# Two FFN down products as seven block products, with the sums for them and for gate and up on GpSimd

## The reference, cut to what matters

```python
D_MODEL = 1024
FFN_DIM = 2816

def swiglu_half(x, pre, post, w_gate, w_up, w_down):
    h = rmsnorm(x, pre)
    y = (jax.nn.silu(h @ w_gate) * (h @ w_up)) @ w_down
    return x + 0.5 * rmsnorm(y, post)

def layer(x, ...):
    h = swiglu_half(x, W['ffn1_pre'], W['ffn1_post'], W['ffn1_gate'], W['ffn1_up'], W['ffn1_down'])
    ...                                    # time mixing, latent attention, memory attention
    y = swiglu_half(h, W['ffn2_pre'], W['ffn2_post'], W['ffn2_gate'], W['ffn2_up'], W['ffn2_down'])
```

## Time and profile before

| | us |
|---|---|
| median of three executions | 3128.83 (3127.26 to 3136.36) |
| the profiled execution, its own time | 3137.18 |
| its span (first to last instruction) | 3135.5 |
| TensorE busy | 2997.9 (96% of the span) |
| VectorE / ScalarE / GpSimd busy | 1674.7 / 1183.5 / 346.8 |
| mean granted clock of TensorE | 0.981 |

### The profile page before, as it was taken

The page is one execution under the profiler, slowest core; times in us unless marked ns, Lnnn a source line. Parts: engine busy times, 40 slices in busy tenths (PEclk is TensorE's granted clock), DMA queues, the critical chain, the costliest instruction groups (busy, mean ns, idle before and its releaser), DMA issues. The chain is left out here.

```text
span 3135.5 us, 63709 instructions
## 1 busy us (share of the span) xinstructions
PE 2997.9 (96%) x26970; PEld 2836.4 (90%) x26970; DVE 1674.7 (53%) x2830; ACT 1183.5 (38%) x2244; POOL 346.8 (11%) x356
## 2 busy tenths in 40 slices
PE   8999999999999988878899989999998999999998
PEld 8999999999999978838777569999998999999998
DVE  7655554554545556566554552343425755565453
ACT  5333334553112233244665351221243433334444
POOL 3000000112001123230003000000015100000111
PEclk9999999999999999989999999999998999999999
DMA  6222237663422120011015641112123222225764
GB/s 173 82 72 73 80 102 230 205 193 108 142 71 68 48 89 4 18 27 45 13 46 166 221 169 51 51 44 61 31 77 99 82 82 82 75 82 176 222 186 138
DMA packets 419542, 312.53 MB, mean 100 GB/s; under 512 B 45720, under 2 KB 391105, under 8 KB 418490
## 3 DMA queue, kind: packets, MB, share of 16 engines
q1 hardware_dynamic: 414394, 288.98, 30.6%
q0 software_dynamic: 3824, 19.47, 1.8%
q10 hardware_dynamic: 1040, 0.00, 0.0%
HBM read 249.20 MB, written 59.21 MB: 98 GB/s over the span
## 5 line engine op out<-in xcount | busy, mean ns | idle before, releaser
L2033 PE MATMUL banks<-hid_pieces,dn_part 128*128 128x344 f32 x3168 | 501.9, 320 | 2.0 <-DVE dn_part L1998 1.3
L2033 PEld LDWEIGHTS banks<-hid_pieces,dn_part 128*128 128x128 f32 x3168 | 498.3, 188 | 3.0 <-DVE dn_part L1998 1.7
L1802 PE MATMUL banks<-x_pieces,gate_pieces 128*128 128x258 f32 x3360 | 414.3, 283 | 0.0
L1802 PE MATMUL banks<-x_pieces,up_pieces 128*128 128x258 f32 x3360 | 414.1, 283 | 0.0
L1802 PEld LDWEIGHTS banks<-x_pieces,gate_pieces 128*128 128x128 f32 x3360 | 408.6, 189 | 0.0
L1802 PEld LDWEIGHTS banks<-x_pieces,up_pieces 128*128 128x128 f32 x3360 | 408.6, 189 | 0.0
L1167 PEld LDWEIGHTS banks<-XR,pR 128*128 128x128 f32 (+1 forms) x1800 | 284.2, 188 | 10.3 <-issue 6.1
L1167 PE MATMUL banks<-XR,pR 128*128 128x344 f32 (+1 forms) x1800 | 289.6, 322 | 3.6 <-DVE pR L2509 2.9
L2012 DVE TENSOR_TENSOR dn_part<-dn_raw,dn_part 128x768 fp32r<-128x768 f32 (+1 forms) x188 | 173.7, 938 | 217.4 <-ACT dn_part L2006 217.4
L1167 PE MATMUL banks<-XR,mg_gate 128*128 128x344 f32 x1728 | 283.3, 319 | 1.3 <-PEq L53 1.3
L1167 PEld LDWEIGHTS banks<-XR,mg_gate 128*128 128x128 f32 x1728 | 273.8, 188 | 1.6 <-issue 1.6
(11 more groups left out here) (523 smaller groups left out, 4744.2 us busy)
## 6 DMA issues: line engine op xcount, KB each, us to landing
dn_raw<-in_ffn_down SPq DMA_DIRECT2D x94, 384.0 KB, 3.5
dn_raw<-in_ffn_down SPq DMA_DIRECT2D x94, 320.0 KB, 3.2
hid_spill<-h_stage SPq DMA_DIRECT2D x44, 516.0 KB, 3.4
hid_raw<-hid_spill SPq DMA_DIRECT2D x24, 688.0 KB, 4.9
praw<-in_w_in SPq DMA_DIRECT2D x24, 512.0 KB, 4.2
sq<-in_w_in SPq DMA_DIRECT2D x24, 512.0 KB, 4.1
tiles<-h_spill SPq DMA_DIRECT2D x8, 1376.0 KB, 8.7
gu_raw<-in_ffn_gate SPq DMA_DIRECT2D x20, 512.0 KB, 4.0
```

What stands on the lines that cost most here:

```text
L1802: ins = k.nc.tensor.matmul(out, self.w[m][:, a, w, f * P:(f + 1) * P], self.x[p][:, b, x, f * TQ:(f + 1) * TQ], start=first and f == 0 and ...
L2033: ins = k.nc.tensor.matmul(k.ps[j][:, 0:TG], w[a][:, f * P:(f + 1) * P], k.hid_pieces[h][:, b, f, :], start=h == 0 and f == 0 and r == 0, ...
```

## The change

- **Down as seven block products.** The output is cut 2 by 2 (tiles 0 to 3 and 4 to 7; columns 0 to 515 and 516 to 1031), and the hidden tiles in even and odd ones. Seven products `m` of the table `DOWN` take the place of eight, in 32 units: units 0 to 23 hold four output tiles of a product for two quarters of 258 columns, the last eight one quarter each. That makes 7 x 4 x 2 x 33 = 1848 matmuls of 258 columns where 1584 of 344 were.
- **Operands for it.** A block product takes weights A11, A12, A22 (blocks of the down weights) or sums S1 to S4 of them, and hidden blocks B11, B21, B22 or sums T1 to T4. `chain` makes, for one pair of hidden tiles, four S or four T on GpSimd: three loads issued by GpSimd itself, three sums with a store to DRAM (`w_sums`, `t_sums`) behind each, a fourth load, a fourth sum and its store. All wait for one another through three buffers. `chains` runs one S and one T chain for each of the 11 iterations, 22 in all, in each FFN.
- **The gate and up weight sums** move from VectorE to GpSimd (`w_sums_pool`), into the same stream; the raw loads now also wait for them.
- **Evictions.** Products 0 and 1 are copied out by ScalarE, products 2 to 6 are added to what is there by VectorE. Squares, norms and the loads around them move to other places (`SQUARES`, `between`), and the split input of the projections gets another layout (`XG`).
- **A new wait of SP**: in `sp_down` the load of the last hidden part of product 1 stands behind `chain_sums.wait(sp, 2 * self.CHAIN)`, all 88 sums of the chains, since that part takes the place of a chain buffer. ScalarE waits for all stores of the chains at unit 5.

```diff
+    H_PARTS = ((0, 0, 5), (0, 5, 9), (0, 9, 11), (1, 0, 6), (1, 6, 11))
     DN_PARTS = ((0, 6), (6, 11))
+    DOWN = (("A11", "B11"), ("A12", "B21"), ("S2", "T2"), ("S3", "T3"), ("A22", "T4"), ("S1", "T1"), ("S4", "B22"))
+    FRESH = (0, 2, 3, 5)
+    UNITS = [(m, j, (0, 1)) for m in range(6) for j in range(4)] + [(6, j, (q,)) for q in range(2) for j in range(4)]
+    LOADED = 28
...
     def load_up(self, sp, it):
         self.w_low[0].wait(sp, 4 * it)
+        self.w_sums[0].wait(sp, 4 * it)
         self.load_raw(sp, 1, it)
...
+    def sp_down(self, sp, between):
...
+        self.hid_stored.wait(sp, 2 * self.N)
+        self.load_down(sp, 4)
+        self.unit_done(sp, 1)
+        for i in (2, 3):
+            self.load_hidden(sp, 1, i)
+        self.chain_sums.wait(sp, 2 * self.CHAIN)
+        self.load_hidden(sp, 1, 4)
+        for u in range(5, self.LOADED):
+            self.unit_done(sp, min(u - 3, 23))
+            self.load_down(sp, u)
+            m = (u - 2) // 4
+            if 6 <= u < 26 and u % 4 in (2, 3):
+                for i in ((0, 1, 2) if u % 4 == 2 else (3, 4)):
+                    self.load_hidden(sp, m + 1, i)
             between(sp, u)
+
+    CHAIN = 4 * (FT // 2)
...
+    def chain(self, pool, i, kind):
...
+        for t in self.chain_stored:
+            t.wait(pool, t.n)
+        for dst, a in zip((x, y, z), src):
+            self.chain_landed.done(pool.dma_start(dst, a))
+        self.chain_landed.wait(pool, self.chain_landed.n)
+        s.done(nc.gpsimd.tensor_tensor(y, x, y, ALU.add if kind == "S" else ALU.subtract))
+        s.wait(pool, at + 1)
+        yz.done(pool.dma_start(out[:, 0, :], y))
+        s.done(nc.gpsimd.tensor_tensor(x, z, x, ALU.subtract))
+        s.wait(pool, at + 2)
+        xs.done(pool.dma_start(out[:, 2, :], x))
...
+        s.wait(pool, at + 3)
+        yz.done(pool.dma_start(out[:, 1, :], z))
+        xs.wait(pool, xs.n)
+        self.chain_landed.done(pool.dma_start(x, src[3]))
+        self.chain_landed.wait(pool, self.chain_landed.n)
+        s.done(nc.gpsimd.tensor_tensor(x, x, z, ALU.subtract))
+        s.wait(pool, at + 4)
+        xs.done(pool.dma_start(out[:, 3, :], x))
+
+    def chains(self, pool):
+        self.w_sums_pool(pool, 0, 1)
+        for i in range(self.N):
+            if i + 1 < self.N:
+                self.w_sums_pool(pool, 1, i + 1)
+            self.hid.wait(pool, 8)
+            self.chain(pool, i, "S")
+            self.hid_stored.wait(pool, 2 * i + 2)
+            self.chain(pool, i, "T")
+            if i + 2 < self.N:
+                self.w_sums_pool(pool, 0, i + 2)
...
-    def w_sums_dve(self, dve, m, it):
+    def w_sums_pool(self, pool, m, it):
...
-        s.done(nc.vector.tensor_tensor(lo[:, 1, 3, :], r21, r22, ALU.add))
+        s.done(nc.gpsimd.tensor_tensor(lo[:, 1, 3, :], r21, r22, ALU.add))
...
-    def unit_pe(self, pe, u):
+    def unit_pe(self, pe, u, between):
...
+        for q in quarters:
+            if m:
+                self.evicted(pe, m - 1, j, q)
+            for i, (first, end) in enumerate(self.DN_PARTS):
+                if u < self.LOADED:
+                    self.dn_low.wait(pe, 2 * u + i + 1)
...
+                        ins = k.nc.tensor.matmul(k.ps[2 * j + q][:, 0:TQ], a[s][:, f * P:(f + 1) * P],
+                                                 k.hid_pieces[m % 2][:, q, f, b, :],
...
     def down_act(self, act, post, between, squared=None):
...
+            if u == 5:
+                self.sums_stored(act)
```

More of the change, by code:

```diff
@@ L1583, in load_gate @@
             self.w_low[1].wait(sp, 4 * (it - 1))
+            self.w_sums[1].wait(sp, 4 * (it - 1))
         self.load_raw(sp, 0, it)
@@ L1916, in problem_dve @@
             self.combine(dve, n - 1, 21)
-        if weights:
-            if s % 2 == 0:
-                self.w_sums_dve(dve, m, of)
-            else:
-                self.w_low_dve(dve, m, of, 2)
-        if n == self.last:
-            self.hidden_low(dve, 0, 0)
+        if weights and s % 2:
+            self.w_low_dve(dve, m, of, 2)
         self.total(dve, n, 11)
         if n == self.last:
-            self.hidden_low(dve, 0, 1)
+            for i in range(2):
+                self.hidden_low(dve, 0, i)
         if s % 2 and weights:
@@ L2021, in unit_pe @@
             self.c12.wait(pe, self.last - 3)
[L2022 to L2034 removed]
+        if u == 3:
+            self.gated(pe, self.last)
@@ L2035, in unit_pe @@
             self.dn.done(ins)
+            if u == 0 and q == 0:
+                self.fourth(pe, self.last)
+            between(pe, u, q if u < 24 else 1)
     def down_pe(self, pe, between):
-        for u in range(48):
-            self.unit_pe(pe, u)
-            if u == 0:
-                self.fourth(pe, self.last)
-            between(pe, u)
-    def evict(self, act, g, j):
-        k = self.k
-        self.dn.wait(act, 2 * (16 * g + 8 + j + 1))
-        self.out.done(k.nc.scalar.activation(k.A[:, j, grp(g)], k.ps[j][:, 0:TG], ACT.Copy))
@@ L2049, in result_ready, with count, unit_of, evicted @@
-    def result_ready(self, eng, g, f):
-        self.out.wait(eng, 8 * g + f + 1)
-    def down_act(self, act, post, between, squared=None):
+        for u in range(len(self.UNITS)):
+            self.unit_pe(pe, u, between)
+    def count(self, u, q):
+        return 2 * u + q + 1 if u < 24 else u + 25
+    def unit_of(self, m, j, q):
+        return 4 * m + j + (4 if m == 6 and q else 0)
+    def evicted(self, eng, m, j, q):
+        if m < 2:
+            self.out.wait(eng, 8 * m + 2 * j + q + 1)
+        else:
+            self.out_dve.wait(eng, 8 * (m - 2) + 2 * j + q + 1 if m < 6 else 32 + 4 * q + j + 1)
```

518 lines of the change are left out of this document (300 added, 218 removed).

## The result

The changed kernel takes 3411.8 us (median of 4 runs, 3407.4 to 3415.9), the kernel before in the same runs 3132.6: a ratio of 1.089 (95% interval 1.086 to 1.092), 279 us slower. The forecast was slower by 148 us, 3280 us, with a range that ended at 3410. The sign and the place were right; the size was not.

A forecast was written before the change was run, and what follows sets the result against it. TensorE bounds the old kernel; GpSimd's stream would bound gate and up. 3137.2 - 53.6 (down) + 180 (loop) + 16 (unit 4) + 8 (ends) = 3288 us profiled, 8.3 less as median: 3280. Range, 8 in 10: 3150 to 3410.

The forecast's parts named there:

- The mechanism: Gate and up: GpSimd's stream becomes the bound, TensorE waits before product 7 once an iteration, period 50.5 us against 40.5.
- The pair of chains, 33.4 us: GpSimd, each iteration: S chain 17.2 and T chain 15.2 us, with sixteen hand-overs 33.4; only 24.5 would fit.
- The hand-over: GpSimd's chains: passing from one instruction to the next costs about 0.06 us, sixteen times a pair.
- The rest of the loop, 6.3 us: Gate and up: from gate sums to next up sums, the raw up load's landing and TensorE's fourth product, 6.3 us.
- rival D: Gate and up: TensorE returns from pauses at the lower clock, 1 to 3 us a period, 3316 us; inside the range.
- The wait at unit 4, 8 us: Start of down: TensorE waits for product 1's last hidden values behind the late chains, 8 us with unit 5, each FFN.
- Down's gain, -26.8: Down: 1848 matmuls of 258 columns, 222.5 us, replace 249.3 us of matmuls; 26.8 us less in each FFN.
- 4 us of ends: End of down: group 1's norm and low pieces come after the last unit, 4 us in each FFN.
- A: Gate and up: GpSimd keeps up, a pair of chains fits in 24.5 us, kernel at 3083 us; chance 0.07.
- B: Chains slowed by DMA traffic or VectorE, 38 us a pair or more, loop 55 and up, 3390 us and above; chance 0.12.
- C: Chains fit, but GpSimd's sums and VectorE's two-input work stretch one another and TensorE waits; 3123 us; chance 0.05.
- The load from GpSimd: Chains: a 256 KB load issued by GpSimd lands after 3.0 us, each further 256 KB behind it adds 0.85.

The follow-up runs named there:

- Experiment 1: Changed kernel with the gate and up weight sums back on VectorE, chains alone on GpSimd: 3236.6 us, 1.031.
- experiment 6: Changed kernel with four buffers a chain instead of three and earlier next loads, gate and up sums still on GpSimd: 3167.5 us, 1.010.
- Experiment 2: Changed kernel without any chains (sums for four of seven products left out), gate and up sums on GpSimd: 3101.1 us, 0.987.
- Experiment 9: Kernel of experiment 8 with the first group's column sums of squares half a unit later in down: 3098.2 us, 0.986.
- experiment 5: Kernel of Experiment 1 with four buffers a chain instead of three and the next chain's loads issued earlier: 3120.7 us, 0.995.
- experiment 3: Changed kernel with the gate sums between the S and the T chain instead of behind both: 3353.2 us, 1.067.
- experiment 8: Kernel of experiment 5 with four steps at the start of down moved: 3108.9 us, 0.989.

## Why the prediction was right or wrong

**The mechanism: right.** Each sign it named is there: a pause before product 7 of the second up problem, ended by ScalarE's copy, behind a split that waits for GpSimd's gate sums; down's matmuls at 0.120 us; a wait at unit 4 for hidden pieces. Experiment 1 removes the pause by taking GpSimd's gate and up sums off its stream, 6 nearly does by making the chains short.

**The pair of chains, 33.4 us: mis-sized, 36.9 in the iteration shown, 37.7 and 36.8 in the mean of the nine iterations of each FFN.** This is the term that failed most: nine times 4.3 and 3.4 us, 69 of the 132 us by which the time is above the forecast. In the iteration shown, counted from an S chain's first issue: the first sum begins at 5.2 (4.7 plus the rest of an issue were forecast), the third store is issued at 11.3 instead of 9.9, the fourth sum ends at 16.9 (14.8) and the next chain begins at 20.1 (17.2). The largest single step is the hand-over, "about 0.06", which I had taken from no row: between a sum and the issue of the store that waits for it lie 0.30 us, four times a chain, 8 x 0.24 = 1.9 us a pair more than costed. The last store holds the next chain back 2.9 us from its issue, not 2.4, and the fourth sum begins 3.3 to 3.8 us after the issue of its load, not 3.0. The sums themselves were right (1.27 to 1.37 against 1.35), and so were the gate and up sums (5.1 against 5.4).

**The rest of the loop, 6.3 us: mis-sized by less, 7.1 in the mean.** This is rival D, which I had set inside the range, at the lower end of its 1 to 3 us: the fourth product comes late by the matmuls at the lower clock (2.95 us for 12 instead of 1.45, then 3.1 to 4.5 for 24 instead of 2.9). In the iteration shown the up loads were issued at 239.1 and 239.5 and, with the median of 5.3 us, were in at about 244.8 (an estimate from these two); the fourth product ended at 246.0. So the clock costs the loop about 1 us a period there. Up sums begin at 79.68 and 576.87 in the first FFN, at 2603.03 and 3092.19 in the second: nine periods of 55.2 and 54.4 us on the average, against 50.5 forecast. That is 9 x (4.7 + 3.9) = 77 us of the 84.6 by which the two stretches up to down exceed the forecast.

**The wait at unit 4, 8 us: mis-sized threefold, 24.4 and 22.6.** The step that failed is "these chains run beside the down loads", to which I gave next to nothing:

```profile
680.42 0.80 PE L2133 MATMUL banks<-hid_pieces,dn_high 128*128 128x258 f32 x2 [24.38 <-DVE hid_pieces L2075]
```

The last four chains took 23.4, 26.9, 22.8 and 16.3 us (the last up to the issue of its last store), the mean traffic from 616 to 700 was 227 GB/s, and the last sum ended 94 us after the last up sums began, where 72 was forecast. I had taken 17.2 us for all four. What the two waits have above 8 us each is 31 of the 132 us. That the heavier traffic made these chains long is likely, but no run takes the down loads away.

**Down's gain, -26.8 and 4 us of ends: nearly right.** Experiment 2 shows -20.1 and -18.2 us a stage against -22.8. A term was missing: TensorE waits for GpSimd's sums of squares four times, 8 us in all, 5.6 of it in down. Experiment 9 took those two waits away, and with them about as much again in clock.

**Rivals.** A had its border at 24.5 us a pair. By the loop's own sum it is 40.5 - 5.1 - 5.1 - 6.3 = 24.0; at 25.4 us a pair (experiment 6) the period is 42.4 to 42.6, so the border is about right. B asked for 38 us a pair, a loop of 55 and up, 10 us and more on top at unit 4, and gave 3390 and above. Measured: 37.7 and 36.8, loops of 55.2 and 54.4, 16 and 15 us on top. So B, at a chance of 0.12, was nearer than the forecast. Its cause, the traffic, fits unit 4; in gate and up about half of what the chains took above my sum is hand-overs, which B didn't have. C is out: it needs chains that fit, and in experiment 5, where they do, VectorE's busy time in the stretch 120 to 440 grew from 189.7 to 244.3 us and TensorE lost 1.4 of 320. The sum for the range's upper side gave 3510, with loads 1.2 us later; I had cut it to 3410 because the traffic of gate and up looked light. It was light (135 GB/s). What lay outside the nearer bound was the hand-over and the length of the chains at the start of down.

**The load from GpSimd.** I took 3.0 us for its landing. By the fit of the Trainium skill (DMA: Bandwidth & Descriptors, Anatomy of one DMA — SWDGE (gpsimd) path) it would be an estimate of 2.6, and the loop 49 us. The traces don't agree: the chain's loads landed at 3.2 us in the median, and at 5.3 in experiment 3.

## What to carry to other kernels

In this kernel a helper engine whose work is load, sum, store cost the landings it waited for one after another, not its arithmetic. Give such a chain one more buffer and issue the next loads early, so that each landing is under another step, before you give the engine other engines' work. An engine that feeds another is a loop: write down the period and what closes it, then ask what the transfers that start at the same moment do to each other once the loop is fast. A price from a quiet stretch was a lower bound here; at a stage's border, where the next stage's loads begin, take the rows of the busiest stretch. Count a wait of the bounding engine with the clock behind it: two waits of 2.8 us cost 10 us in experiment 8.
